# Sample attention of a latent-attention decoder step: eight samples singly, or two waves of four on 32 array columns each

## The reference: what is computed

```python
# per sample: q_lat (4 tokens, 8 heads, 256), q_rope (4, 8, 64)
# keys: 1024 past rows, paged, and the sample's 4 new rows
s = einsum('bthc,bsc->bhts', ql, ckv) + einsum('bthr,bsr->bhts', qr, krope)
s = where(k_pos <= q_pos, s * SOFTMAX_SCALE, -inf)
p = softmax(s)
o_lat = einsum('bhts,bsc->bthc', p, ckv)   # then w_uv per head, and w_o
```

## Time and profile before

| | us |
|---|---|
| median of 3 runs (2006.75 to 2009.55) | 2007.27 |
| profiled execution, device time | 2006.67 |
| its span, first to last instruction | 2005.1 |
| PE busy in the span | 1825.3 (91%) |
| DVE busy | 1217.3 (61%) |
| ACT busy | 922.2 (46%) |
| sample attention, 731.17 to 892.00 | 160.83 |
| experts, 981 to the end | 1024 |

### The profile page before, as it was taken

One profiled execution on the slowest core, in us unless ns is written; L12 is line 12 of the kernel. 1 busy time (PEld: TensorE's weight loads), 2 busy tenths in 40 slices (PEclk: granted clock), 3 DMA queues, 4 the chain that ended last, 5 costly groups with the idle time before them and its releaser, 6 DMA issues.

```text
span 2005.1 us, 23401 instructions
## 1 busy us (share of the span) xinstructions
PE 1825.3 (91%) x8410; PEld 1402.3 (70%) x8410; DVE 1217.3 (61%) x1254; ACT 922.2 (46%) x802; POOL 91.2 (5%) x156
## 2 busy tenths in 40 slices
PE   5998969999979878888699999999999999999993
PEld 3746657999955543347587787877878778787783
DVE  2102684444344332223588888888888888888886
ACT  1100022443201111102377777777777677777774
POOL 2000020001001002200100000000000000000001
PEclk9995569999989568898799999999999999999997
DMA  9640042434724002202399999999999999999993
GB/s 271 237 178 1 0 48 98 163 98 128 222 85 173 8 0 63 69 14 105 125 372 365 356 370 341 387 365 356 368 343 386 359 363 368 345 380 354 374 368 135
DMA packets 220336, 458.37 MB, mean 229 GB/s; under 512 B 11045, under 2 KB 45418, under 8 KB 220282
## 3 DMA queue, kind: packets, MB, share of 16 engines
q1 hardware_dynamic: 209034, 428.96, 59.8%
q0 software_dynamic: 9968, 28.12, 5.0%
q10 hardware_dynamic: 1280, 0.54, 0.2%
HBM read 440.29 MB, written 17.30 MB: 228 GB/s over the span
## 4 chain that ended last, share of the span: by engine, by line
PE 82%; DVE 8%; ACT 5%; issue 3%; DMA 1%; POOL 0%; SPq 0%; POOLq 0%; ACTq 0%; DVEq 0%
PE bank L374 15%; PE bank L376 15%; PE bank L375 15%; PE bank L370 8%; ACT wpart L1542 3%; PE wide L376 2%; PE wide L374 2%; PE wide L375 2%; PE bank L733 2%; DVE wpart L892 2%; PE wide L716 2%; PE bank L774 2%; PE bank L546 1%; PE bank L678 1%; PE wide L848 1%
## 5 line engine op out<-in xcount | busy, mean ns | idle before, releaser
L892 DVE TENSOR_TENSOR wpart<-mring,wpart 128x2048 fp32r<-128x2048 f32 x339 | 775.6, 2290 | 158.3 <-ACT wpart L1542 157.5
L1542 ACT ACTIVATE wpart<-mring 128x2048 fp32r<-128x2048 f32 x336 | 643.1, 1917 | 202.9 <-PE bank L376 109.7
L374 PE MATMUL bank<-wpart,xgp 128*128 128x512 f32 x896 | 361.0, 403 | 6.7 <-DVE wpart L892 5.1
L375 PE MATMUL bank<-wpart,xgp 128*128 128x512 f32 x896 | 354.7, 396 | 0.0
L376 PE MATMUL bank<-wpart,xgp 128*128 128x512 f32 x896 | 354.6, 396 | 0.0
L374 PEld LDWEIGHTS bank<-wpart,xgp 128*128 128x128 f32 x896 | 168.8, 188 | 49.9 <-DVE wpart L892 10.2
L376 PEld LDWEIGHTS bank<-wpart,xgp 128*128 128x128 f32 x896 | 168.7, 188 | 40.9
L375 PEld LDWEIGHTS bank<-wpart,xgp 128*128 128x128 f32 x896 | 169.0, 189 | 37.9
L374 PE MATMUL bank<-ffparts,wpart 128*128 128x288 f32 (+1 forms) x528 | 159.2, 301 | 5.2 <-DVE ffparts L892 4.2
L376 PE MATMUL bank<-ffparts,wpart 128*128 128x288 f32 (+1 forms) x528 | 157.4, 298 | 0.0
L375 PE MATMUL bank<-ffparts,wpart 128*128 128x288 f32 (+1 forms) x528 | 155.1, 294 | 0.0
(11 more groups left out here) (347 smaller groups left out, 2143.7 us busy)
## 6 DMA issues: line engine op xcount, KB each, us to landing
mring<-in_w_gate_m SPq DMA_DIRECT2D x114, 1024.0 KB, 5.3
mring<-in_w_up_m SPq DMA_DIRECT2D x113, 1024.0 KB, 5.7
mring<-in_w_down_m SPq DMA_DIRECT2D x112, 1024.0 KB, 5.3
ring<-in_w_in_a SPq DMA_DIRECT2D x6, 2048.0 KB, 24.3
ring<-in_w_down_d SPq DMA_DIRECT2D x8, 1344.0 KB, 7.1
ring<-in_w_gate_d SPq DMA_DIRECT2D x5, 2048.0 KB, 9.0
ring<-in_w_up_d SPq DMA_DIRECT2D x5, 2048.0 KB, 7.9
xs<-arena POOLq DMA_DIRECT2D x4, 1664.0 KB, 17.3
```

The lines of the kernel that those rows point to most:

```text
L374: pe.matmul(o, a[0], b[0], start=start, stop=False)
L375: pe.matmul(o, a[1], b[0], start=False, stop=False)
L892: return v.tensor_tensor(dst, src, high.bitcast(F32), ALU.subtract)
L1542: a.activation(wpart[:, stage(h), 0, :], mring[:, place(h % IH), :], ACT.Copy).then_inc(S["hi_ready"], 1)
```

## The change

The samples are taken in two waves of four (`WAVES`, `WB`). Sample `b` of a wave writes its scores to partitions 32 b to 32 b + 31 of `wide`, and so its stationary operand of 32 columns lies in another quarter of the array; the four samples' products stand next to each other in the program. Pages are turned in quarters: a turn `t` (eight in all) takes two pages of each of the wave's four samples, again in six groups of four pieces, into one of two buffers (`turnT`), and `s_scores(t)` multiplies the four samples' 256 keys. Softmax, the turns of the probabilities (now full 128 x 128 pieces, copied by DVE from bank 4 and by ACT from bank 2) and the turn back run once per wave, on 128 partitions. PE's order of turns (T), scores (S), probabilities (P), attend (A) and turn back (U) is written out:

T0 T1 S0 T2 S1 T3 S2 T4 S3 T5 P0 S4 A0 T6 S5 U0 T7 S6 S7 P1 A1 U1.

All 64 pages have a place of their own, in slots 0 to 4. SP loads them in one stretch before `wo1`, each sample's after the chunk under it is released (`under_page`); then halves 1 to 4 after wave 0's attend, `wo1` and half 0 after wave 1's, halves 5 and 6 when `wo1` is released. POOL's rotary loads follow the same releases, four samples ahead of its stores and four behind.

```diff
-BUFS = 3
+WAVES, WB = 2, 4
+QK = 256
+STEPS = PAST // QK
+TGROUPS = 6
...
-        cacheT = area(10176, CT, PAST)
-        cacheR = area(12224, PAST, rows=ROPE)
+        PTS = area(16320, NPG + 1, WB * TS)
+        turnT = [area(at, CT + 1, WB, QK) for at in (10176, 13248)]
...
+        nat = ring[:, 0:5, :].rearrange("p s n -> p (s n)").rearrange("p (k n) -> p k n", k=NB)
+        pagebuf = [nat[:, k, :] for k in (2, 3, 4, 5, 0, 1, 6, 7)]
+        under_page = ["dkv", "dq", "uk", "uk", "uq0", "uq0", "uq1", "uq1"]
...
-            def s_scores(b):
+            def s_scores(t):
+                w, qd = divmod(t, STEPS)
+                pe.wait_ge(S["tpa_free"], 3 * (t + 1))
+                pe.wait_ge(S["tpd_free"], 3 * (t + 1))
...
+                kv = turnT[t % 2]
+                for k in range(CT):
+                    for b in range(WB):
+                        pe.matmul(wide[b * TS:(b + 1) * TS, qd * QK:(qd + 1) * QK], qls[:, k, w * WB + b, :], kv[:, k, b, :],
+                                  start=(k == 0), stop=False)
+                for b in range(WB):
+                    ins = pe.matmul(wide[b * TS:(b + 1) * TS, qd * QK:(qd + 1) * QK], qrs[:, w * WB + b, :], kv[0:ROPE, CT, b, :],
+                                    start=False, stop=True)
+                ins.then_inc(S["part_done"], 1)
...
+            def s_attend(w):
+                pe.wait_ge(S["pt_ready"], NU + 2 * (w + 1))
+                pe.wait_ge(S["pta_ready"], w + 1)
                 for pg in range(NPG + 1):
...
+                    for b in range(WB):
+                        kv = ctk[w * WB + b][:, pg, :] if pg < NPG else ctok[0:TS, 2, 0:CKV]
+                        rows = P if pg < NPG else TS
+                        ins = pe.matmul(bank[3][b * TS:(b + 1) * TS, 0:CKV], PTS[0:rows, pg, b * TS:(b + 1) * TS], kv,
+                                        start=(pg == 0), stop=(pg == NPG))
                 ins.then_inc(S["av_full"], 1)
...
+            def cache_evac(t):
+                if t >= 2:
+                    a.wait_ge(S["part_done"], t - 1)
...
+            for n, (name, parts) in enumerate(chunks):
+                if name == "wo1":
+                    sp.wait_ge(S["ld_pages"], 16)
+                    for b in range(NB):
+                        sp.wait_ge(*release[CH[under_page[b]]])
+                        load_cache(b)
+                    sp.wait_ge(S["av_full"], 1)
+                    for h in range(1, 5):
+                        expert_half(0, h)
+                    sp.wait_ge(S["av_full"], 2)
...
+            expert_half(0, 0)
+            sp.wait_ge(*release[CH["wo1"]])
+            expert_half(0, 5)
+            expert_half(0, 6)
```

## The result

The changed kernel takes 1897.91 us (median of four runs, 1896.16 to 1903.52) against 2007.93 for the kernel before on the same chip (2006.75 to 2009.55): a ratio of 0.9456, 95% interval 0.9435 to 0.9478. I had said 1917.4, range 1909 to 1946. The sign and the mechanism of the sample attention were right and the time was not: 19.5 us more came off than forecast, and the range does not hold it.

The account below looks back on a forecast made before the run. PE's own work plus its waits was taken to bound the sample attention. Stage terms summed to 71.9 us against 160.8; with 1.0 from loads, 2006.67 - 89.9 = 1916.8, stated as 1917.4 for the runs' median, range 1909 to 1946.

Parts of the forecast that it names:

- move as a block: Everything behind the sample attention, experts included: released by PE's results and not by a time, so its length was kept.
- The stage: Sample attention, first turned page to first value product: 71.9 us forecast against 160.8, a gain of 88.9.
- Turns: Turning the pages on PE in eight turns, 35.6 us in all: 5.3, 4.3, five of 3.9, and 6.5 for turn 5.
- Scores: Score products, four column groups beside each other: 1.6 us a quarter, 0.4 a wave for new keys, 13.6 in all.
- Attend: Products of probabilities with pages: 18 passes deep per wave, 4.19 us each, 8.4 in all.
- two, or one, at a time: Rivals: column groups overlap only in part; two at a time 1936.5 us, chance 0.09; one at a time 1974.8, chance 0.05.
- drained groups: Rival: each change of column group empties the array, 0.38 us a pass, + 108.5, 2025.9 us; chance 0.04.
- Softmax: Softmax and ends: PE idles 2.76 us in wave 1, end 1.4, wave 0's turn back 0.3; together 4.5 us.
- Clock: Granted clock 0.50 for 6.83 us behind a softmax wait, one spell a wave on dense work: 6.8 us.
- The rule that spoke against it: Weight loads overlap products only where row groups differ; as rival, 84 steps show their loads, + 9.2, 1926.6 us; chance 0.04.
- Loads: All 64 pages, wo1 and the halves arrive without a wait; SP needs 11.5 us for eight pages.
- The 1.0 us of the earlier trace: PE's wait of 1.00 us at 513.27 goes, as pages of samples 0 and 1 no longer delay w_down_d; gain 1.0.

Follow-up runs that it names:

- after_early_copy: The kernel after, with ScalarE's copy of the first group of the sixth quarter's turned keys moved ahead of wave 0's exponential; 1895.45 us, ratio 0.9437.
- after_wpart32: The kernel after, with wpart 32 bytes further and 96 bytes more behind it, so xgp lies at 212480; 1918.39 us, ratio 0.9551.
- before_const4: The kernel before, with four columns of zeros more among its constants, so every tensor behind them lies where after has it; 1991.57 us, ratio 0.9916.
- before_move32: The kernel before, with 32 more bytes per partition left free ahead of xgp, so xgp and hhp start where after has them; 1988.49 us, ratio 0.9899.
- after_scan: The kernel after, plus 64 cells of 24 passes on PE alone behind the expert stage, at varied weight and stream offsets; 2255.91 us (a single run).

## Why the prediction was wrong, and where it was right

**The step that failed** is the last sentence of the first paragraph of the prediction: "I let all that follows the sample attention move as a block". It argued that the experts' work is released by results and not by a time. That is true, and it did not suffice: the layout of SBUF is no time and no release either. Of the 20.6 us by which the profiled execution lies below the 1916.8 of the sum, the expert stage gives 20.7. The rest nearly cancels: the sample attention took 2.4 us less than the sum has, the stretch between it and the experts 0.4 less, and it all began 3.0 later. The diff showed the cause in one line, the 60 columns of the mask that became 64, and I had costed it at nothing without asking what moves behind it. No rival held it, so the range had no room for it. That the block moved otherwise is so: from the value product to the first expert pass there are 88.9 us after and 89.3 before.

**The stage** was right, 69.5 against 71.9, and term by term:
- *Turns.* T0 and T1 9.5 us (733.18 to 742.67; forecast 9.6). A turn with its scores 5.5 (744.24 to 749.75; 3.9 + 1.6).
- *Scores* 1.57 a quarter; forecast 1.6. *Attend* 4.15 in wave 0; forecast 4.19. The rivals of two, or one, at a time and of drained groups are out: 72 passes in 4.15 us are 58 ns each.
- *Softmax.* PE's idle time in wave 1 is 3.07 us; forecast 2.76. The wait for the copies of the probabilities is 0.56; forecast 0.6.
- *Clock.* Two spells of 6.83 us where the forecast had them, but they cost 4.0 us instead of 6.8: turn 5 takes 7.24 where 6.5 were put, the probabilities 2.06 and 2.2 for 1.2, scores 0.1 more, the second attend 5.5 for 4.19. In 0.8 us of the first spell and 2.0 of the second PE was idle, waiting for ACT, and that part cost nothing. The 2.8 us that this saved are more than the stage's 2.4; the other terms gave 0.4 back, most of it in the two waits of wave 1's softmax and end (0.3 and 0.2). In after_early_copy the first spell goes with its wait, as the sum had tied the two.

**The rule that spoke against it.** The weight loads of L759 last 110 ns (shortest, median and longest of 128 below), and 72 passes with their 72 loads take 4.15 us, as long as 18 with 18. The loads are hidden.

```profile
L759 PEld LDWEIGHTS bank<-ring,arena x128: 106/110/178, 772.3 to 799.9; 128*32 128x32 f32 x128
```

The Trainium skill ("TensorE: Matmul & The Clock Gate", Part 3: Packing small matmuls) lets a weight load overlap running products only where its row group differs. For four column groups on the same rows the trace does not agree: one load of 110 ns shown in each of the 84 steps would have been 9.2 us.

**Loads** were hidden as said. SP's pages went out in one stretch (timeline of SP in after):

```profile
577.05 105.07 SPq L1725 DMA_DIRECT2D ring<-in_cache_ckv  x64
```

That is to 682, 13.1 us for eight pages instead of 11.5, and still 51 us ahead of the first turn. Neither a wave nor the output products waited.

**The 1.0 us of the earlier trace rows** is a small miss. The wait at 513.27 is gone from after, yet the first turn starts 2.0 us later than before, not 1.0 earlier. 1.1 us of this stood already at the first pass of the dense layer (334.5 against 333.4; the other kernels of this study, before's and after's alike, have 334.1 to 336.7). The dense layer should then have gained the 1.0 us and lost 0.3 instead (216.4 us from its first pass to its last, against 216.1): its 1584 passes of 288 columns follow each other after 133.3 ns (mean, from 345 us on), where before they did after 132.2. That is the layout again. after_wpart32, which is after with a shift alone, has 132.2, and before_const4, which is before with four columns of zeros, has 133.3. The weights lie in `wpart` here and the stream in `ffparts`, which starts where the arena does, behind `cs`. Counted as for the experts, weights less stream modulo 256, the distance is 32 in before and before_move32, 160 in after_wpart32, and those three have 132.2; it is 0 in all the others, and they have 133.3. (The streams step by 1152 bytes, so every other one lies 128 further.) No run set this distance by itself, so that it counts here is a fit and not shown. The last 0.7 us, between the dense layer and the first turn, I did not track down.

## What to carry to other kernels

When a diff changes the size of any buffer, list what is allocated behind it, and ask of every hot loop of products whether its weights and its stream moved against each other: here that was worth 20.7 us, almost a quarter of the stage's own gain of 91.4, and the shift alone takes 1% off the old kernel. Then measure: the distance of 0 that was the fast one for the experts' passes of 512 columns goes with the slower pace in the dense layer's passes of 288. Products of 32 output columns go four for the price of one, if the program issues the four groups in turn; the same products group by group gain nothing. A wait of 2.5 us on PE can cost more than itself: here a spell of halved clock went with it, and the stage became 3.7 us shorter without it. So a copy that PE waits for belongs ahead of a longer instruction in ACT's queue.

## What the runs showed of the hardware

- A pass of 512 columns whose weights start at the same place modulo 256 bytes as the operand that streams takes 226.7 ns in after_scan, at other distances 228.9 (192) to 234.2 (96); steps of 32 bytes were tried, on operands of type float32r, with all weight tiles and streams at steps of 512 bytes. PE alone shows it, so it needs no other engine's work. Why is not known: the weight load's own duration (median) is 187 to 188 ns in fast and slow cells alike. For passes of 288 columns the layout matters too (132.2 or 133.3 ns), and there 0 is not the fast distance.
- Four column groups on all 128 rows lose next to nothing when their products come in turn: 1.57 us for four samples' scores against 1.53 for one. Group by group the same products take 6.11.
